# Moving three blocks of a conditioning product within the output-projection stage

## The reference

```
mod = silu(c) @ w_ada + b_ada               # 6 x 1024 values per conditioning vector, two vectors
shift1, scale1, gate1, shift2, scale2, gate2 = split(mod, 6)
h  = rmsnorm(x) * (1 + scale1) + shift1
...                                         # input projection, attention, RWKV-7, two branch projections
x  = x + gate1 * (merged @ w_out)
h2 = rmsnorm(x) * (1 + scale2) + shift2
up_u, up_g = split(conv3(h2 @ ffn_up), 2)
x  = x + gate2 * ((silu(up_g) * up_u) @ ffn_down)
y  = rmsnorm(x)
```

## Time and profile before

| | us |
|---|---|
| median of three runs | 1453.39 |
| the profiled execution, device time | 1453.39 |
| its span, first to last instruction | 1451.6 |
| PE busy (matmul) | 1327.4 (91%) |
| DVE busy | 731.2 (50%) |
| ACT busy | 529.5 (36%) |

### The profile page before, as it was taken

The page is one execution under the profiler, slowest core; times in us unless marked ns, Lnnn a source line. Parts: engine busy times, 40 slices in busy tenths (PEclk is TensorE's granted clock), DMA queues, the critical chain, the costliest instruction groups (busy, mean ns, idle before and its releaser), DMA issues.

```text
span 1451.6 us, 31774 instructions
## 1 busy us (share of the span) xinstructions
PE 1327.4 (91%) x13955; PEld 1223.6 (84%) x13955; DVE 731.2 (50%) x1087; ACT 529.5 (36%) x795; POOL 41.8 (3%) x84
## 2 busy tenths in 40 slices
PE   4799999997999799969993989999999999989996
PEld 2699999997997465559983978789999999989995
DVE  3517742634554489955535542265454545434534
ACT  3635534422334343313333222264343333333433
POOL 0000011000000000000001000000000000000000
PEclk9899999999999799989996999999999999999998
DMA  9222265314000200020006467211221212022222
GB/s 395 82 95 97 94 268 173 105 46 161 8 4 3 87 0 0 1 96 8 4 3 243 149 245 300 97 59 64 81 78 66 87 58 65 15 63 75 65 74 93
DMA packets 24761, 134.58 MB, mean 93 GB/s; under 512 B 2992, under 2 KB 3632, under 8 KB 16208
## 3 DMA queue, kind: packets, MB, share of 16 engines
q1 hardware_dynamic: 19088, 103.59, 20.2%
q0 software_dynamic: 5568, 29.40, 5.3%
HBM read 112.66 MB, written 20.32 MB: 92 GB/s over the span
## 4 chain that ended last, share of the span: by engine, by line
PE 83%; DVE 8%; ACT 3%; DMA 3%; issue 2%; PEld 1%; POOLq 0%; PEldq 0%; POOL 0%; SPq 0%; DVEq 0%; ACTq 0%
PE ps L675 45%; PE ps L1125 11%; PE ps L838 4%; PE ps L826 3%; PE ps L806 2%; PE ps L1025 2%; PE ps L984 1%; PE ps L818 1%; DMA xT<-in_x 1%; DVE rden L1807 1%; PE ps L700 1%; PE ps L1002 1%; PE ps L710 1%; PE ps L949 1%; DMA bld<-branch_scratch 1%
## 5 line engine op out<-in xcount | busy, mean ns | idle before, releaser
L675 PE MATMUL ps<-h2lo,whi 128*128 128x322 f32 x672 | 154.5, 311 | 0.7 <-ACT facc L1225 0.7
L675 PE MATMUL ps<-h2hi,wlo 128*128 128x322 f32 x672 | 155.0, 312 | 0.0
L675 PE MATMUL ps<-h2hi,whi 128*128 128x322 f32 x672 | 154.0, 310 | 0.0
L1517 DVE TENSOR_TENSOR wlo<-raw,whi 128x2048 fp32r<-128x2048 f32 x48 | 109.7, 2288 | 72.2 <-ACT whi L1187 72.2
L675 PE MATMUL ps<-hlo,whi 128*128 128x322 f32 x544 | 127.8, 316 | 1.0 <-ACT qkv L1251 1.0
L675 PE MATMUL ps<-hhi,wlo 128*128 128x322 f32 x544 | 125.4, 312 | 0.0
L675 PE MATMUL ps<-hhi,whi 128*128 128x322 f32 x544 | 124.7, 310 | 0.0
L675 PEld LDWEIGHTS ps<-h2hi,whi 128*128 128x128 f32 x672 | 114.2, 190 | 0.0
L675 PEld LDWEIGHTS ps<-h2lo,whi 128*128 128x128 f32 x672 | 113.0, 189 | 0.9 <-DVE wlo L1517 0.9
L675 PEld LDWEIGHTS ps<-h2hi,wlo 128*128 128x128 f32 x672 | 113.7, 189 | 0.0
L1561 DVE SCALAR_TENSOR_TENSOR facc<-fraw,par,facc 128x642 f32<-128x642 f32 x44 | 39.1, 888 | 138.7 <-ACT facc L1225 138.7
(11 more groups left out here) (313 smaller groups left out, 2637.7 us busy)
## 6 DMA issues: line engine op xcount, KB each, us to landing
raw<-in_wblk SPq DMA_DIRECT2D x48, 1024.0 KB, 4.9
adl<-in_wada SPq DMA_DIRECT2D x8, 2048.0 KB, 8.2
raw<-in_wdn SPq DMA_DIRECT2D x44, 256.0 KB, 2.6
adaw<-in_wada SPq DMA_DIRECT2D x4, 2048.0 KB, 17.6
gate_scratch<-gout POOLq DMA_DIRECT2D x16, 322.0 KB, 2.5
gld<-gate_scratch POOLq DMA_DIRECT2D x8, 644.0 KB, 4.2
attention_inputs_used<-attention_scratch SPq DMA_DIRECT2D x1, 5056.0 KB, 14.6
u_scratch<-uout POOLq DMA_DIRECT2D x12, 320.0 KB, 2.5
```

Source lines behind the costliest of these rows:

```text
L675: mm = pe.matmul(o, w, v, start=first, stop=last and w is hi and x is xh[n])
L1517: TT(wlo[s][:, :], raw[s][:, :], whi[s][:, :].bitcast(F32), ALU.subtract).then_inc(lo_done, 1)
```

## The change

On PE, the first late block (4) is now placed behind the wait for all eight merged parts (`m_lo`), where it stood ahead of it, behind the wait for the last branch tile's reading. Block 5 follows directly, ahead of tile 0, where it stood behind tile 0. Block 11 and the turns of blocks 10 and 11 move from behind the last sum of squares into `between_out(6)` and `between_out(7)`. ACT copies block 11's row instead of DVE, and DVE adds the bias to all three remaining vectors (shift2, scale2, gate2: 24 columns) in one instruction behind the eighth tile, where it did two of them behind the seventh tile and the last behind `modulate`.

```diff
-        pe.wait_ge(tile_evac, 2 * BLK_OUT + 2)
+        pe.wait_ge(m_lo, KD)
         ada_late(4)
-        pe.wait_ge(m_lo, KD)
+        ada_late(5)
 
         def between_out(t):
 
             if t == 0:
-                ada_late(5)
                 ada_turn(4)
                 ada_turn(5)
             else:
-                if t < 6:
+                if t < 7:
                     ada_late(t + 5)
-                if 1 < t < 6:
+                if t > 1:
                     ada_turn(t + 4)
                 x1_squares(t - 1)
...
         x1_squares(KD - 1)
-        ada_late(11)
-        pe.wait_ge(mod_done, 2)
-        ada_turn(10)
-        ada_turn(11)
         pe.wait_ge(tile_evac, 2 * BLK_UP + 2)
         dense_first(BLK_UP, KD, h2hi, h2lo)
...
         for k in range(KD):
-            if 1 <= k < 6:
+            if 1 <= k < 7:
                 ada_row(k + 5)
             x1_squares(k)
...
-            if o == 6:
-                dv.wait_ge(modt_done, 9)
-                st.last(mod_columns(24, 16, 5, 16))
-                one_plus(sc2g, 32, "g2").then_inc(mod_done, 1)
-        dv.wait_ge(ada_done, 12)
-        dv.tensor_copy(adrow[1][:, :], bank(4)).then_inc(row_done, 1)
+        dv.wait_ge(modt_done, 11)
+        st.last(mod_columns(24, 24, 5, 16))
+        one_plus(sc2g, 32, "g2").then_inc(mod_done, 1)
         modulate(1, x1, h2hi, h2lo)
-        dv.wait_ge(modt_done, 11)
-        st.last(mod_columns(40, 8, 5, 48))
         TS(g2h[:, :, :], modT[:, 40:40 + KD, :], 0.5, None, ALU.mult)
```

## The result

The changed kernel takes 1462.98 us (median of five runs, 1460.68 to 1463.70) against 1454.46 us of the kernel before (five runs, 1453.28 to 1456.34). The ratio is 1.0052, with a 95% interval of 1.0037 to 1.0066: slower by 5.4 to 9.6 us. The forecast was 1459.7 us, with a range up to 1462.0: the direction was right, the size short, and the measured time lies outside the range. The ratio forecast, 1.0043, lies inside the measured interval.

A forecast was written before the change was run, and what follows sets the result against it. PE was taken to bound the stage, except in two waits set by DVE and ACT. Terms 1.85 + 0.72 + 2.94 + 0.1 + 0.65 = 6.3 us on 1453.4 gave 1459.7 us, own range 1457.6 to 1461.6, 8-in-10 range 1456.9 to 1462.0.

The forecast's parts named there:

- Block 4 behind the wait: At the output projection's start, block 4 leaves the wait for the merged parts, where it was hidden: +1.85 us.
- the copy wait: Ahead of tile 0, block 5 shares bank 4 with block 4 and must wait for ACT's copy: +0.72 us.
- the round behind tile 6: Block 11 and turn 10 make this round like the four before it, 11.18 instead of 8.24 us: +2.94 us.
- turn 11 in ACT's gap: Behind tile 7, PE's idle time for ACT's square covers the 0.98 us turn but for 0.3 at most: +0.1 us.
- the nothing for the tail: Behind the last sum of squares, the removed PE work and DVE copy were hidden: 0, bounds 0 to -0.3 us.
- a late landing: Rival: block 5's weights land after the copy, adding some 2 us, 1462 us; chance 0.13 shared with a longer slow stretch.
- a tail that was not free: Rival: PE's 3.8 us or DVE's copy in the tail held the modulation back; 1455.9 us at the most, chance 0.04.
- The clock at the head: Behind the wait for the merged parts, 4.5 us at 1.2 GHz lose 1.8 instead of 1.7 us: +0.1 us.
- For the tail the step: Behind the wait before the up projection, 4.5 us at 1.2 GHz lose 2.25 instead of 1.7 us: +0.55 us.
- The last rival: A longer slow stretch at both places, 1461.6 to 1463 us; chance 0.13, shared with late weights for block 5.
- The point it was measured from: The sum was added to the profiled execution before the change, 1453.39 us, taken as also the median of the runs.
- The rule of the Trainium skill: Idle gaps of PE between matmul bursts halve the clock; so neither 1.2 GHz stretch goes away and no -1.7 us term applies.

The follow-up runs named there:

- the two kernels without slow clock: The kernel before and the changed kernel, each with products nobody reads put into PE's waits of this stage; ratios 0.9979 and 1.0025.
- before_filled: The kernel before, with products nobody reads put into PE's waits ahead of and behind block 4 and in the tail; ratio 0.9979, median 1451.66 us.
- the 68 products: Kernel before with unread products only in PE's waits of the first 50 us, 68 of them behind the first turns; 1461.59 us, ratio 1.0046.
- after_look2: The changed kernel unedited, one more single execution with a profile; 1462.97 us.
- after_head_filled: The changed kernel with products nobody reads (10 and 28) only in the wait at the head; 1459.12 us, ratio 1.0030 against the kernel before.

## Why the prediction was short

**The moved work: right.** Block 4 behind the wait, the copy wait (0.81 us for 0.72), the round behind tile 6, turn 11 in ACT's gap: 5.6 us by the sum, 5.52 us between the two kernels without slow clock. Block 5's weights were in time in every profile of the changed kernel (0.81 us of idle in each, block 4 slow or not), the nothing for the tail was right, and the rivals of a late landing and of a tail that was not free fell.

**The clock at the head: this is the step that failed.** The mechanism was right and its size was not. The step said that of 4.5 us at 1.2 GHz little is left for block 5, 1.8 us in all against 1.7 before. The profiles show 98.82 - 97.13 = 1.7 us in two executions and 100.5 - 97.13 = 3.4 us in the other two, against 1.6 before. The term was +0.1 and should have been 0.1 or 1.8. The slow stretch behind the wait was 4.0 to 4.3 us or 7.8 to 7.9 us long, the second beyond the upper bound of "5.3 us or a little over", and in that case the first block and the copy wait do not use it up. I had taken the mean of two rows, 3.7 and 5.3 us, for a thing with two values, though in these rows the longer wait (8.46 us) had the shorter stretch, so they gave no ground for going between them. That the profiled execution after met the forecast of 5.7 us at the up projection's start is in part luck: it shows the short case. For the tail the step had 2.25 us against 1.7, while B shows 0.8 to 1.5 against 1.0: the 4.5 us of slow time were about right (4.5 and 4.2 us in the two short cases, 3.0 in the two long ones), but the price of half of it was too large on both sides, since the up projection's first block is paced by DVE and ACT, but the difference, predicted +0.55, came out between -0.2 and +0.5. In all the clock adds 0.5 us in two of the profiles and 1.6 us in two, where the sum had 0.65: A and B together are 6.1 or 7.2 us longer. The last rival, a longer slow stretch at both places with 1461.6 to 1463 us and part of a chance of 0.13, names what came, but at one place only.

**The point it was measured from: 1.1 us off.** The sum was made against an execution of 1453.39 us, "which is also the median of the runs". With three runs it was; with 35 the median is 1454.59 us and they reach from 1449.9 to 1457.5. That execution had h1 at 50.29 us where two later profiles have 51.70 and 52.23, and took 2.3 and 2.6 us less, of which h1 accounts for 1.4 and 1.9 us. The range had no term for this. Of the 3.3 us between forecast and result, 1.1 us is the reference point, about 1 us the clock (7.2 against 6.3 us, where the long case holds), and the rest, some 1.2 us, is within what five runs leave open and has no cause shown.

**The rule of the Trainium skill** weighed in the prediction (no idle gaps between bursts, "TensorE: Matmul & The Clock Gate", section "Why this matters for your kernels") was borne out: the stretch at 1.2 GHz stayed at both places (granted clock 0.60 and 0.67 in the windows after, 0.79 before). And it reaches further than I used it. In the kernel before, the waits are worth 2.6 us in A and B together, by before_filled, and that is a gain that can be had.

## What to carry to other kernels

Work that stands in a wait of the matrix engine is free there and costs its full length anywhere on the engine's own chain: before moving it, find in the timeline whether the idle time beside it has another engine as releaser. Emptying a wait can cost a second time through the clock (by -0.2 to +0.5 us at the tail here, by 0.1 or 1.8 us at the head), and a following chain of short, mutually waiting pieces can stay in the slow stretch to its end; filling it with products nobody reads gave 0.2% here, and 0.45% with the start filled too. But a filler that begins with the clock already down can run slowly to its end and overrun the wait, as the 68 products did, for a loss of 0.46%. And one profiled execution is a ruler for differences within it, not for the level: cut several profiles at points that an edit cannot touch before trusting a difference of a few us.

## What the runs showed of the hardware

The same ada block, sixteen records of a 32-column product in the profile, took 1.92 or 1.93 us or 3.58 to 3.64 us in this stage wherever it stands apart, with the granted clock at 1.00 or 0.50. Products of 128 columns with their own weight load took 0.217 us each behind the first turns (68 in 14.77 us, granted clock 0.50) and 0.115 us each ahead of the first squares (62 in 7.14 us, granted clock 1.00). In the first of these stretches PE was busy for 14.5 us and the clock did not rise.

A slow stretch of PE in front of work that DVE and ACT feed cost less than half its length. The granted clock of the 8 us behind the start of the up projection was 0.81, 0.79, 0.72 and 0.61 in after_look2, before, after and after_head_filled, which is 3.0, 3.4, 4.5 and 6.2 us at 1.2 GHz; B was longer than the 14.18 us of the filled kernels by 0.8, 1.0, 1.5 and 2.25 us. In front of dense tiles and ada blocks it cost the half (1.6 us for 3.4 us in the kernel before).
